# A two-layer recurrent trunk with routed experts: the first expert's rows by a matmul, logits by token tiles, earlier weight loads

## The chip, the core and the metric

The kernel runs on one core of a Trainium2 chip. The metric is the device time of one execution in microseconds. All arithmetic is fp32.

## What is computed

256 prompt tokens and 8 sample tokens, each a row of 1024 values, pass two layers. A layer is a mixer, a LayerNorm, a mixture of experts and another LayerNorm; each sublayer f gives x <- LayerNorm(alpha * x + f(x)). Layer 0's mixer is gated DeltaNet and mLSTM heads with one output projection (w_out); layer 1's is a state-space layer (S5) and a gated linear unit, (g @ A) * sigmoid(g @ B). The experts are:

```
logits = x @ router_w                       # 16 experts
probs = softmax(logits); sel = probs + router_b
grp_score = sum of the top 2 of each group of 4 in sel; best = argmax(grp_score)
idx = top 2 of sel within the best group; wts = probs[idx] / sum
out = sum over experts e of comb[e] * ((silu(x @ gate[e]) * (x @ up[e])) @ down[e])
```

## The kernel before

**Tiles.** Tokens are in three tiles: 0 and 1 (128 rows each, every second token) and TT = 2, the 8 samples. The five engines have programs of their own, at the end of the file, and meet at semaphores.

**Projection and LayerNorm.** In layer 0 `mix_pe_out` (L776) adds the output projection to the scaled residual, tile 0, tile 1 (L804), samples (L816). `ln_dve` (L1418) norms each tile, in that order, on DVE (VectorE); a tile is ready after L1442. In layer 1 `glu_pe` (L2457) computes tile 0, tile 1, then the samples (L2478, both halves of the columns), and `glu_half` takes the halves into the residual.

**Routing.** PE (TensorE) transposes tiles 0 and 1 (`xT_pe`); DVE and ACT (ScalarE) copy them from PSUM. `route_pe` (L1528) then multiplies the router by all 256 columns at once (L1533) into logits with experts on partitions, transposes these back (L1538) and treats the samples apart (L1513, L1541). `route_dve` (L1564) has some 60 small DVE operations in a chain: softmax, best group, first and second expert, the mask of both (L1639). Two matmuls count the tokens ahead in each expert (L1546, L1547). From this come each token's slot (`at_slot`) and list (`in_list`); each expert has a list of up to 64 rows. `list_value` (L1693) goes through a matmul (L1551) into row numbers (`gidx`), and `list_sel` through another (L1556) into the weights of the combination. GpSimd (POOL) copies the normed rows with columns permuted (`rows_pool`, L1716), SyncE stores them to DRAM (L1723), and `pool_gather` (L1903) fetches an expert's rows by an indirect DMA (L1911).

**Experts.** `moe_pe` (L1963) takes the 16 experts in order: gate and up (L1803, L1804, eight chunks each in two passes), the next expert's rows transposed (`pe_tokens`, L1782), the former expert's down projection (L1827), the hidden rows transposed (`pe_units`), and for every second expert the combination (L1845). Before expert 0 it waits for `sel` and puts down tile 0's residual (L1481).

**Weights.** An expert has 4 MB of gate and up weights and 2 MB of down weights. Gate and up have three places, loaded in halves, down two (layer 0) or three (layer 1). SyncE's queue issues the loads in one fixed order and waits in it for the place to be freed: `moe_first_loads` (L2037) and `moe_weights` (L2063). In layer 0 the loads for experts 0 and 1 wait for the samples' projection (the step `mixAB2`), gate and up of expert 3 for expert 0's matmuls, and the third down load for expert 0's down matmuls (`down_done`, L1775). `keep_busy` (L302) issues 512-column matmuls whose results nobody reads.

## Time and profile before

| | us |
|---|---|
| median of 3 runs (1001.24 to 1004.36) | 1003.9 |
| the profiled execution | 1003.38 |
| its span | 1001.6 |
| PE busy | 902.1 (90%) |
| DVE busy | 400.7 (40%) |
| DMA moved | 277.52 MB, 277 GB/s mean |

Busy shares are means over stages. The prediction reads stages by windows, queues and timelines. PEclk is TensorE's granted clock, 1.00 for 2.4 GHz and 0.50 for 1.2 GHz. A PE timeline row merges neighbouring instructions of one line; an fp32 matmul stands as two, called passes here.

### The profile page before, as it was taken

What the parts mean: (1) busy time and instruction counts of PE and PEld (TensorE: products, weight loads), DVE (VectorE), ACT (ScalarE), POOL (GpSimd) and SP (SyncE); (2) the same over time, 40 slices, a digit from 0 to 9 for tenths busy, and PEclk for the clock granted to TensorE, in tenths of its full rate; (3) what the DMA queues carried; (4) which work ended last, traced back from release to release, by engine and by line L of the source; (5) the groups of instructions that cost most, each with busy time, mean ns of one, the idle gap of its engine ahead of it and who ended that gap; (6) DMA issues with size and microseconds to landing.
All of it is one profiled execution on the core that took longest, in us unless ns stands there. A gap on an engine that the chain in (4) does not pass through costs nothing.

```text
span 1001.6 us, 12283 instructions
## 1 busy us (share of the span) xinstructions
PE 902.1 (90%) x4936; PEld 490.6 (49%) x4936; DVE 400.7 (40%) x838; ACT 175.7 (18%) x310; POOL 217.7 (22%) x328
## 2 busy tenths in 40 slices
PE   7999988998984799999899879899749999999993
PEld 5888867996343233333333368744233333333331
DVE  4599507726646022122134279602561121221115
ACT  0402140223010111111011153301301111111011
POOL 4579982401021411101010110100211001111000
PEclk8999997999896899999999999999869999999997
DMA  9446739102769579999999936660479789999982
GB/s 269 106 134 256 261 121 306 67 12 98 258 216 408 200 303 409 406 403 401 410 406 425 419 122 198 207 268 0 190 311 368 307 357 406 397 415 398 417 340 87
DMA packets 83579, 277.52 MB, mean 277 GB/s; under 512 B 25337, under 2 KB 44231, under 8 KB 60854
## 3 DMA queue, kind: packets, MB, share of 16 engines
q1 hardware_dynamic: 70298, 255.86, 66.3%
q10 hardware_dynamic: 10660, 16.49, 5.0%
q0 software_dynamic: 2560, 4.33, 1.5%
q8 instruction: 42, 0.69, 0.3%
q14 instruction: 19, 0.16, 0.0%
HBM read 261.49 MB, written 18.01 MB: 279 GB/s over the span
## 4 chain that ended last, share of the span: by engine, by line
PE 73%; DMA 15%; DVE 7%; ACT 2%; issue 1%; SPq 0%; POOL 0%; DVEq 0%; ACTq 0%; POOLq 0%
PE ps L1803 17%; DMA ring<-in_moe_w_up 13%; PE ps L342 11%; PE ps L1827 8%; PE ps L2471 6%; PE ps L1845 4%; PE ps L804 3%; PE ps L1782 3%; PE ps L2333 1%; PE ps L305 1%; PE ps L633 1%; PE ps L1533 1%; PE ps L650 1%; DMA work<-x_rows,work 1%; PE ps L2348 1%
## 5 line engine op out<-in xcount | busy, mean ns | idle before, releaser
L1803 PE MATMUL ps<-ring,work 128*64 128x512 f32 x480 | 217.3, 605 | 11.4 <-DMA ring<-in_moe_w_up 9.9
L1804 PE MATMUL ps<-ring,work 128*64 128x512 f32 x480 | 217.4, 605 | 0.0
L1803 PEld LDWEIGHTS ps<-ring,work 128*64 128x64 f32 x480 | 63.8, 139 | 137.5 <-issue 121.4
L1887 DVE TENSOR_TENSOR work<-ps,work 64x512 f32<-64x512 f32 x32 | 33.8, 1057 | 223.3 <-ACT work L1858 223.3
L342 PE MATMUL ps<-work,ring 128*128 128x264 f32 x512 | 115.2, 387 | 0.0
L1827 PE MATMUL ps<-ring,work 128*64 128x512 f32 x248 | 113.0, 598 | 1.5 <-DVE work L1892 1.4
L1828 PE MATMUL ps<-ring,work 128*64 128x512 f32 x248 | 113.1, 599 | 0.0
L342 PEld LDWEIGHTS ps<-work,ring 128*128 128x128 f32 x512 | 96.8, 190 | 16.4
L1249 POOL TENSOR_TENSOR ring<-ring 128x512 f32<-128x512 f32 (+5 forms) x76 | 90.5, 1207 | 9.5 <-DVE ring L1245 6.2
L1897 DVE COPY work<-ps 64x512 f32<-64x512 f32 x32 | 22.2, 694 | 149.8 <-PE ps L1828 149.8
L1908 POOL COPY work<-work 64x1 int32<-64x1 int32 x32 | 5.7, 178 | 339.6 <-PE ps L1782 300.0
L1782 PEld LDWEIGHTS ps<-const,work 64*128 64x128 f32 x448 | 39.3, 162 | 52.4 <-issue 44.1
L1804 PEld LDWEIGHTS ps<-ring,work 128*64 128x64 f32 x480 | 63.8, 139 | 0.0
L1845 PE MATMUL ps<-work 128*128 128x512 f32 x128 | 59.5, 605 | 2.0 <-DVE work L1897 1.8
L1858 ACT ACTIVATE work<-ps 64x512 f32<-64x512 f32 x32 | 18.8, 589 | 239.0 <-PE ps L1804 239.0
L2471 PE MATMUL ps<-ring,work 128*128 128x512 f32 x128 | 57.1, 608 | 3.0 <-ACT work L2414 2.1
L1827 PEld LDWEIGHTS ps<-ring,work 128*64 128x64 f32 x248 | 31.4, 136 | 57.5 <-issue 54.0
L1782 PE MATMUL ps<-const,work 64*128 64x64 f32 x448 | 48.2, 246 | 6.3 <-DMA work<-x_rows,work 4.3
L2471 PEld LDWEIGHTS ps<-ring,work 128*128 128x128 f32 x128 | 24.7, 195 | 34.2 <-issue 30.8
L1845 PEld LDWEIGHTS ps<-work 128*128 128x128 f32 x128 | 22.9, 189 | 37.8 <-issue 37.8
L504 DVE SCALAR_TENSOR_TENSOR work<-work 128x256 f32<-128x256 f32 x36 | 40.4, 1123 | 1.3
L1854 ACT COPY work<-ps 128x512 f32<-128x512 f32 x32 | 18.7, 585 | 108.5 <-PE ps L1782 108.5
(491 smaller groups left out, 1187.8 us busy)
## 6 DMA issues: line engine op xcount, KB each, us to landing
ring<-in_moe_w_down SPq DMA_DIRECT2D x31, 2048.0 KB, 17.0
ring<-in_moe_w_gate SPq DMA_DIRECT2D x60, 1024.0 KB, 14.6
ring<-in_moe_w_up SPq DMA_DIRECT2D x60, 1024.0 KB, 16.8
ring<-in_w_in ACTq DMA_DIRECT2D x6, 2048.0 KB, 8.7
s_out_mats<-ring SPq DMA_DIRECT2D x4, 1280.0 KB, 4.7
ring<-in_w_in SPq DMA_DIRECT2D x2, 2048.0 KB, 10.2
s_in_mats<-ring SPq DMA_DIRECT2D x4, 1024.0 KB, 6.3
ring<-in_w_out SPq DMA_DIRECT2D x1, 4096.0 KB, 16.5
```

What stands on the lines that cost most here:

```text
L342: last = nc.tensor.matmul(ps[:, proj_bank(j), 0:T], win[g % 2][:, k, (j % 4) * P:(j % 4 + 1) * P], xT[:, k], start=k == 0, stop=k == DC - 1)
L504: nc.vector.scalar_tensor_tensor(y, raw[:, c, w:w + SEQ], convT[:, c, 24 + w:25 + w], y, ALU.mult, ALU.add).then_inc(*dv.done())
L804: last = nc.tensor.matmul(ps[:, 2 * i + n, :], rows_of(oT[:, k], i), wout[:, k, n * 512:(n + 1) * 512], start=False, stop=k == 7)
L1249: tt = lambda o, a, b, op, name=None: nc.gpsimd.tensor_tensor(o, a, b, op).then_inc(*po.done(name))
L1782: last = op(bank[:, c * SLOT:(c + 1) * SLOT], rows[0:SLOT, c * P:(c + 1) * P], ident[0:SLOT, 0:SLOT], **(dict(start=True, stop=True) if c ...
L1803: nc.tensor.matmul(ps[0:SLOT, 5, :], xgT[s][:, c], gate_w[slot][:, c], start=c == 0, stop=c == DC - 1)
L1804: last = nc.tensor.matmul(ps[SLOT:P, 5, :], xgT[s][:, c], up_w[slot][:, c], start=c == 0, stop=c == DC - 1)
L1827: nc.tensor.matmul(ps[0:SLOT, 7, :], hidT[s][:, c], down_w[l][slot][:, c, 0:512], start=c == 0, stop=c == 3)
L1828: last = nc.tensor.matmul(ps[SLOT:P, 7, :], hidT[s][:, c], down_w[l][slot][:, c, 512:D], start=c == 0, stop=c == 3)
L1845: last = nc.tensor.matmul(ps[:, 2 * i + n, :], S[rows, i * P:(i + 1) * P], y[rows, 512 * n:512 * n + 512], **flags)
L1887: nc.vector.tensor_tensor(hid[s][0:SLOT].rearrange("t (c p) -> t p c", c=4), strided(ps[SLOT:P, 5, :]), strided(sg[s][SLOT:P]), ALU.mult). ...
L2471: last = nc.tensor.matmul(ps[:, banks_ab[ab], :], gyT[:, k, i * P:(i + 1) * P], glu_w(h, k)[:, ab], start=k == 0, stop=k == DC - 1)
```

## The change

- Output projection: tile 0, samples, tile 1. Gated unit: half 0 of tiles 0, 1 and the samples, half 1 of the samples, of tile 0, of tile 1. The norm's order is 0, TT, 1 in layer 0 and TT, 0, 1 in layer 1.
- Logits come per tile, with tokens on partitions: the transposed tile is the stationary operand, the router the moving one. All PSUM copies of the transposed tiles are on ACT. Group scores are the largest of six pair sums.
- Six `keep_busy` matmuls follow the logits, two follow the counts. The counts of tiles ahead are accumulated in PSUM.
- Expert 0's rows are no longer gathered: `pe_first_tokens` multiplies the permuted rows, as POOL leaves them, by a one-hot matrix of its slots (24 matmuls). The gathers start with expert 1. The matmuls of `sel` and tile 0's residual move behind expert 0's gate and up. The largest count goes to `route_sel` behind expert 0's product, too.
- Expert 0's gate and up weights are loaded in four 1 MB pieces, each when the chunks of w_out or of the gated unit's weights that lie there have been used. In layer 1 expert 1's come earlier still.

```
-                        pe_outer(t, 2 + k // 5)
+            residual_pe(t, 0, 0)
+            pe_outer(t, 1)
+            for k in range(8):
+                for n in range(2):
+                    last = nc.tensor.matmul(ps[:, n, :], rows_of(oT[:, k], 0), wout[:, k, n * 512:(n + 1) * 512], start=False, stop=k == 7)
...
+            t.wait_ge(*dv.at("new11"))
+            residual_pe(t, 1, 2)
             t.wait_ge(*dv.at("new15"))
             residual_pe(t, TT, 4)
...
+            for k in range(8):
+                for n in range(2):
+                    last = nc.tensor.matmul(ps[:, 2 + n, :], rows_of(oT[:, k], 1), wout[:, k, n * 512:(n + 1) * 512], start=False, stop=k == 7)
+                if k == 7:
+                    last.then_inc(*pe.done("mixAB1"))
+                elif k % 2 == 1:
+                    last.then_inc(*pe.done(f"wout{k // 2}"))
...
+
...
+        def logits_pe(t, tag, i):
+
+            t.wait_ge(*ac.at(f"{tag}xT_in{i}"))
+            rows = slice(i * P, i * P + tok(i))
+            for k in range(DC):
+                last = nc.tensor.matmul(ps[0:tok(i), 1, i * NE:(i + 1) * NE], xT[:, k, rows], router[:, k], start=k == 0, stop=k == DC - 1)
+            return last
...
         def route_pe(t, tag):
-            t.wait_ge(*ac.at(f"{tag}xT"))
-            t.wait_ge(*dv.at(f"{tag}xT"))
+            xT_pe(t, tag, 0)
+            xT_rest_pe(t, tag)
             t.wait_ge(sem("router_in"), 32)
-            for k in range(DC):
-                last = nc.tensor.matmul(ps[0:NE, 6, 0:SEQ], router[:, k], xT[:, k, 0:SEQ], start=k == 0, stop=k == DC - 1)
-            last.then_inc(*pe.done(f"{tag}logitsT"))
...
-            for k in range(DC):
-                last = nc.tensor.matmul(ps[0:NS, 1, TT * NE:3 * NE], xT[:, k, SEQ:], router[:, k], start=k == 0, stop=k == DC - 1)
-            last.then_inc(*pe.done(f"{tag}logits"))
+            logits_pe(t, tag, 0)
+            logits_pe(t, tag, TT)
+            xT_pe(t, tag, 1)
+            logits_pe(t, tag, 1).then_inc(*pe.done(f"{tag}logits"))
+            keep_busy(0, 6)
             t.wait_ge(*dv.at(f"{tag}mask"))
             flat_mask = rt(9, 48)
...
+            nc.tensor.matmul(ps[:, 1, 0:48], before, flat_mask, start=True, stop=False)
+            t.wait_ge(*dv.at(f"{tag}tiles_so_far"))
+            nc.tensor.matmul(ps[:, 1, 0:48], ones, rt(4, 48), start=False, stop=True).then_inc(*pe.done(f"{tag}pos"))
+            t.wait_ge(*dv.at(f"{tag}all_tiles"))
+            nc.tensor.matmul(ps[:, 6, 256:256 + NE], ones, rt(5, 48)[:, 0:NE], start=True, stop=True).then_inc(*pe.done(f"{tag}total"))
+
+            keep_busy(0, 2)
             t.wait_ge(*dv.at(f"{tag}lists"))
             for n in range(6):
                 last = nc.tensor.matmul(ps[0:SLOT, 1, 128:128 + LISTS], at_slot[:, n], list_value[:, n], start=n == 0, stop=n == 5)
             last.then_inc(*pe.done(f"{tag}lists"))
+
+        def route_sel_pe(t, tag):
+
             t.wait_ge(*dv.at(f"{tag}list_sel"))
...
-            for i, (a, b, op) in enumerate(((0, 1, ALU.max), (0, 1, ALU.min), (2, 3, ALU.max), (2, 3, ALU.min))):
...
+            pair, score = rt(4, 12, 6), rt(13, 48)[:, 0:12]
+            for at, n, step in ((0, 3, 1), (3, 2, 2), (5, 1, 3)):
+                nc.vector.tensor_tensor(pair[:, :, at:at + n], g4[:, :, 0:n], g4[:, :, step:step + n], ALU.add).then_inc(*dv.done())
+            v.wait_ge(*dv.last())
+            red(score, pair, ALU.max).then_inc(*dv.done())
...
-            inside = rt(6, 12, EPG)
-            nc.vector.tensor_copy(inside, g_hot.unsqueeze(2).to_broadcast([P, 12, EPG])).then_inc(*dv.done())
-            v.wait_ge(*dv.last())
-            nc.vector.tensor_tensor(sel, sel, rt(6), ALU.mult).then_inc(*dv.done())
-            nc.vector.tensor_scalar(rt(6), rt(6), 1e30, -1e30, ALU.mult, ALU.add).then_inc(*dv.done())
-            v.wait_ge(*dv.last())
-            nc.vector.tensor_tensor(sel, sel, rt(6), ALU.add).then_inc(*dv.done())
+            outside = rt(5, 48)[:, 0:12]
+            nc.vector.tensor_scalar(outside, g_hot, 1e30, -1e30, ALU.mult, ALU.add).then_inc(*dv.done())
+            v.wait_ge(*dv.last())
+            nc.vector.tensor_tensor(g4, g4, outside.unsqueeze(2).to_broadcast([P, 12, EPG]), ALU.add).then_inc(*dv.done())
...
+            so_far, mask = rt(4), rt(9)
+            nc.vector.memset(so_far[:, 0], 0.0).then_inc(*dv.done())
+            v.wait_ge(*dv.at(f"{tag}mask"))
+            nc.vector.tensor_copy(so_far[:, 1], mask[:, 0]).then_inc(*dv.done())
+            nc.vector.tensor_tensor(so_far[:, 2], mask[:, 0], mask[:, 1], ALU.add).then_inc(*dv.done(f"{tag}tiles_so_far"))
...
+            nc.vector.tensor_tensor(rt(5, 48)[:, 0:NE], so_far[:, 2], mask[:, 2], ALU.add).then_inc(*dv.done(f"{tag}all_tiles"))
...
+                red(at[:, 1, :, j], rt(12 + j), ALU.add).then_inc(*dv.done())
             v.wait_ge(*pe.at(f"{tag}pos"))
-            pos = rt(6)
-            nc.vector.tensor_copy(rt(12, 96), ps[:, 1, 0:96]).then_inc(*dv.done())
-            v.wait_ge(*dv.last())
...
+            pos = ps[:, 1, 0:48].rearrange("p (a b) -> p a b", a=3)
...
             nc.vector.tensor_tensor(list_value, in_list, per_list(value_f), ALU.mult).then_inc(*dv.done(f"{tag}lists"))
...
+            nc.vector.tensor_tensor(first_slots, at_slot,
+                                    in_list[:, :, 0:1].to_broadcast([P, 6, SLOT]), ALU.mult).then_inc(*dv.done())
+            v.wait_ge(*dv.last())
+            nc.vector.tensor_tensor(first_slot[:, :, 0], first_slot[:, :, 0], first_slot[:, :, 1], ALU.add).then_inc(*dv.done(f"{tag}first_slot"))
...
+            route_lists(v, tag)
...
+        def route_sel(v, tag):
+
+            v.wait_ge(*pe.at(f"{tag}total"))
+            nc.vector.tensor_reduce(cnt[:, 0:1], ps[:, 6, 256:256 + NE], AX, ALU.max).then_inc(*dv.done())
+            v.wait_ge(*dv.last())
+            nc.vector.tensor_copy(cnt[:, 1:2].bitcast(I32), cnt[:, 0:1]).then_inc(*dv.done(f"{tag}cnt"))
             v.wait_ge(*pe.at(f"{tag}sel"))
             nc.vector.tensor_copy(sel.rearrange("p a b -> p (a b)"), ps[:, 0, 0:2 * LISTS]).then_inc(*dv.done(f"{tag}sel"))
...
+        def pe_first_tokens(t, tag, l):
+
+            for i in range(3):
+                t.wait_ge(*po.at(f"{tag}rows{i}"))
+            t.wait_ge(*dv.at(f"{tag}first_slot"))
+            for c in range(DC):
+                for i in range(3):
+                    n = tok(i)
+                    last = nc.tensor.matmul(ps[:, 4, c * SLOT:(c + 1) * SLOT], xperm[0:n, i, c * P:(c + 1) * P], first_slot[0:n, i, 0],
+                                            start=i == 0, stop=i == 2)
+            last.then_inc(sem(f"tokens_done{l}"), 1)
+
...
-            pool.wait_ge(*x_ready(tag, 2))
-            for s in range(2):
-                nc.gpsimd.memset(xg[s], 0.0).then_inc(*po.done(f"{tag}xg_zero"))
-            pool.wait_ge(*po.at(f"{tag}xg_zero"))
+            pool.wait_ge(*x_ready(tag, 1))
+            nc.gpsimd.memset(xg[1], 0.0).then_inc(*po.done(f"{tag}xg_zero1"))
+            pool.wait_ge(*po.at(f"{tag}xg_zero1"))
             pool.wait_ge(*dv.at(f"{tag}gidx"))
             pool.wait_ge(sem(f"x_rows{l}"), 48)
-            for k in range(NE):
+            for k in range(1, NE):
+                if k == 2:
+                    pool.wait_ge(*pe.at(f"{tag}sel"))
+                    nc.gpsimd.memset(xg[0], 0.0).then_inc(*po.done(f"{tag}xg_zero0"))
+                    pool.wait_ge(*po.at(f"{tag}xg_zero0"))
                 pool_gather(pool, l, *at_expert(k))
...
-            t.wait_ge(*dv.at(f"{tag}sel"))
-            residual_pe(t, 0, 0)
-            pe_tokens(t, l, *at_expert(0))
+            pe_first_tokens(t, tag, l)
             for k in range(NE):
                 pe_gate_up(t, l, *at_expert(k))
+                if k == 0:
+                    route_sel_pe(t, tag)
                 if k % 2 == 1 and k >= 3:
                     pe_combine(t, l, k // 2 - 1, k - 2, slice(0, P), (k // 2 - 1) % 2)
...
+                if k == 0:
+                    t.wait_ge(*dv.at(f"{tag}sel"))
+                    residual_pe(t, 0, 0)
...
+            a.wait_ge(*dv.at(f"{tag}list_sel"))
...
+        def first_gate_up(q, l, freed):
+
+            for part, (dst, name) in enumerate(((gate_w[0], "moe_w_gate"), (up_w[0], "moe_w_up"))):
+                for half in range(2):
+                    q.wait_ge(*freed[2 * part + half])
+                    cols = slice(half * 4 * FF, (half + 1) * 4 * FF)
+                    q.dma_start(dst.rearrange("p k f -> p (k f)")[:, cols].unsqueeze(1),
+                                io[name][l].rearrange("e (p k) f -> p e (k f)", p=P)[:, 0:1, cols]).then_inc(sem(f"w_gu{half}0_{l}"), 16)
+
         def moe_first_loads(q, l):
...
                 gate_up_load(q, l, *load_of(2))
             else:
-                q.wait_ge(*pe.at("glu2"))
-                gate_up_load(q, l, *load_of(0))
+                q.wait_ge(*pe.at(f"glu0{TT}"))
                 gate_up_load(q, l, *load_of(1))
+                first_gate_up(q, l, [pe.at(f"glu_b{min(b, 2)}") for b in range(4)])
+                q.wait_ge(*pe.at("glu11"))
+                down_load(q, l, *load_of(1))
                 route_loads(q, "n2", l)
-                down_load(q, l, *load_of(1))
-                q.wait_ge(*pe.at("n2sel"))
+                q.wait_ge(*pe.at("n2logits"))
                 q.wait_ge(sem("stores_s5"), 16 * 2 * (NS + 1))
                 down_load(q, l, *load_of(2))
...
+            glu_tile_pe(t, 0, 0)
+            s5_state_pe(t)
+            glu_tile_pe(t, 0, 1)
+            glu_samples_pe(t, 0)
+            for b in range(4):
+                t.wait_ge(sem(f"glu_in1{b}"), 64)
+            t.wait_ge(*ac.at("tanh00"))
+            glu_samples_pe(t, 1)
+            t.wait_ge(*ac.at("s5_states"))
+            glu_tile_pe(t, 1, 0)
+            t.wait_ge(*dv.at("prod00"))
+            glu_tile_pe(t, 1, 1)
...
+            ln_root(act, "n0", 0)
             act.wait_ge(*pe.at("mixAB2"))
             sample_rows(act, "n0", 4)
             ln_root(act, "n0", TT)
-            xT_copy(act, ac, nc.scalar.copy, "n0", 1)
+            ln_root(act, "n0", 1)
+            xT_copy(act, "n0", 0)
+            xT_rest_copy(act, "n0")
+            xT_copy(act, "n0", 1)
...
+            for i in ROWS["n2"]:
+                glu_act(act, 1, i)
                 ln_root(act, "n2", i)
-            xT_copy(act, ac, nc.scalar.copy, "n2", 1)
+            xT_copy(act, "n2", 0)
+            xT_rest_copy(act, "n2")
+            xT_copy(act, "n2", 1)
...
+            ln_dve(dve, "n0", 1, in_banks, mixed, ROWS["n0"])
             route_dve(dve, "n0")
-            route_lists(dve, "n0")
```

## Rows read from the trace of the kernel before

**Rows 1.** Windows: start:end, length, busy (x instructions) per engine, PEclk, DMA share, GB/s.

```profile
326.00:339.00 13.00, 8.42 (x31) 3.19 (x31) 0.00 (x0) 1.87 (x2) 6.49 (x15) 0.74 0.15 45
...
350.50:356.00 5.50, 5.50 (x32) 2.03 (x28) 1.07 (x1) 1.18 (x2) 1.32 (x3) 1.00 0.15 50
...
371.00:552.00 181.00, 174.42 (x860) 64.90 (x856) 48.30 (x84) 21.02 (x36) 13.18 (x30) 0.99 1.01 408
...
808.00:965.00 157.00, 153.42 (x768) 57.43 (x766) 28.50 (x44) 19.27 (x33) 11.84 (x27) 1.00 1.01 405
```

**Rows 2.** SyncE's queue in layer 0: start us, us, line, transfer.

```profile
291.68 0.35 SPq L1766 DMA_DIRECT2D ring<-in_moe_w_gate  x1
...
338.74 0.33 SPq L1766 DMA_DIRECT2D ring<-in_moe_w_gate  x1
...
356.01 0.33 SPq L1776 DMA_DIRECT2D ring<-in_moe_w_down  x1
```

**Rows 3.** PE in layer 0: start us, us, line, operation, count, idle before.

```profile
273.61 13.90 PE L804 MATMUL ps<-ring,work 128*128 128x512 f32 x32
...
297.43 6.44 PE L1533 MATMUL ps<-work,fix 128*16 128x256 f32 x16 [3.48 <-ACT work L2163]
303.81 0.66 PE L1513 MATMUL ps<-const,work 8*128 8x8 f32 x8
...
304.79 0.56 PE L1541 MATMUL ps<-fix,work 128*8 128x16 f32 x16
313.64 0.66 PE L1546 MATMUL ps<-work,fix 128*128 128x48 f32 x2 [8.30 <-DVE work L1639]
...
319.78 1.73 PE L1551 MATMUL ps<-work 128*64 128x80 f32 x11 [5.04 <-DVE work L1693]
...
332.82 1.11 PE L1803 MATMUL ps<-ring,work 128*64 128x512 f32 x1 [0.68 <-ACT work L1854]
...
344.50 0.64 PE L1803 MATMUL ps<-ring,work 128*64 128x512 f32 x1
```

**Rows 4.** PE: the first gate matmul of layer 1's first expert.

```profile
752.13 0.64 PE L1803 MATMUL ps<-ring,work 128*64 128x512 f32 x1 [0.68 <-ACT work L1854]
```

**Rows 5.** DVE in layer 0, the same columns.

```profile
268.49 4.22 DVE L994 SCALAR_TENSOR_TENSOR ring<-ring,work,ps 128x128 f32<-128x128 f32 x16 [2.21 <-PE ps L772]
...
290.58 1.29 DVE L1442 SCALAR_TENSOR_TENSOR work<-work 128x1024 f32<-128x1024 f32 x1
...
313.38 0.21 DVE L1639 TENSOR_TENSOR work<-work,fix 128x48 f32<-128x48 f32 x1
...
319.06 0.66 DVE L1693 TENSOR_TENSOR work<-work,fix 128x480 f32<-128x480 f32 x1
```

**Rows 6.** Windows of the granted clock, columns as in the first group.

```profile
296.20:303.00 6.80, 5.57 (x14) 2.01 (x15) 2.53 (x5) 1.75 (x2) 3.80 (x3) 0.51 1.01 424
303.00:306.00 3.00, 2.24 (x30) 1.40 (x28) 1.12 (x6) 0.00 (x0) 0.00 (x0) 0.97 1.02 429
307.00:323.00 16.00, 4.31 (x29) 4.15 (x31) 13.11 (x70) 0.00 (x0) 0.36 (x2) 0.50 1.01 400
...
719.40:726.20 6.80, 4.99 (x12) 1.80 (x13) 3.06 (x6) 1.71 (x2) 3.67 (x3) 0.52 1.01 426
```

**Rows 7.** The chain of waits in time: start us, us, what.

```profile
177.78 0.89 PE ps L646 x8
...
598.94 5.20 PE ps L305 x12
```

**Rows 8.** PE: the first gate matmul of layer 1's second expert.

```profile
761.60 0.64 PE L1803 MATMUL ps<-ring,work 128*64 128x512 f32 x1
```

**Rows 9.** Gathers of both layers, issue to landing.

```profile
DMA to landing us min/median/max: 3.0/7.3/10.1
```

**Rows 10.** PE in layer 1: the gated unit's samples, the last logits.

```profile
706.23 7.05 PE L2478 MATMUL ps<-ring,work 128*8 128x512 f32 x64
...
728.30 0.56 PE L1541 MATMUL ps<-fix,work 128*8 128x16 f32 x16
```

225 lines of the change are left out of this document (88 added, 137 removed).

## The prediction

> **What bounds the kernel now.** I read four views. First the windows, to see which resource is full in each stage of the experts. In layer 0 the DMA engines are idle from 326 to 339 us and nearly so from 350.5 to 356, and then full for 181 us at 408 GB/s, while PE is busy 174.4 of the 181; in layer 1 they are full from 808 to 965 [rows 1]. So the late part of both layers is set by the stream of weights, and PE has only a few us to spare: both must come forward for the end to come forward.
>
> Then SyncE's queue, to see what starts that full stream. In layer 0 expert 3's first half is issued at 338.74, after half of expert 0's gate and up, and the third down load at 356.01, after expert 0's down matmuls; from there the stream never stops [rows 2]. In layer 1 the full stretch begins at 808 [rows 1] in the same way, with a load that waits for a half of the fifth expert's gate and up. Neither start is set by the first loads, which are issued at 291.68 [rows 2] and have landed by 326 [rows 1]. Both are set by when PE begins the experts. The time to shorten is therefore from the last norm to the first gate matmul, which runs at 332.82 [rows 3] and 752.13 [rows 4]; a us saved there moves PE and the stream alike.
>
> Last the timelines of PE and DVE in between. Tile 1 is normed at 291.87 [rows 5], the logits end at 305.35 (304.79 + 0.56) [rows 3], the mask at 313.59, `list_value` at 319.72 [rows 5]; then come the list matmuls, the gather and the transposes. The granted clock is 0.51 in 296.2:303 and 0.50 in 307:323, where PE does little [rows 6].
>
> **Prices.** A pass with a 128-column stationary tile and few moving columns is 0.111 us at full clock (0.89 / 8) [rows 7]; two at half clock take 0.66 with their drain [rows 3], and I take twice the warm price, 0.22. A 512-column pass is 0.433 (5.20 / 12) [rows 7]. Eight passes with 8 contraction rows take 0.57 (303.81 to 304.38, 0.66 with the drain) [rows 3] at clock 0.97 [rows 6]: 0.071 each. A dependent DVE step is 0.19 (13.11 / 70) [rows 6], one that follows without a wait about 0.1.
>
> The trace thus makes a load with 8 rows cheaper than one with 128. The Trainium skill says otherwise (TensorE: Matmul & The Clock Gate, LDWEIGHTS): load time goes by columns, not by contraction rows, P / 1.2, so 107 ns either way. By that page the 16 sample passes of the new product cost an estimated 1.7 instead of 1.1 us, and the result is 1.2 us later over both layers. I stay with the row.
>
> **Layer 0, part by part.**
> 1. Order of the projection. The same matmuls run: samples between the tiles, tile 1 last. Tile 1's 13.90 us [rows 3] now end where the samples did, at 291.6 (their step released the issue at 291.68) [rows 2]. Its norm took 4.4 us (287.51 to 291.87) [rows 3, 5], so it is ready at 296.0. The wait for `new15`, now ahead of the samples, costs nothing: those states were done at 272.71 (268.49 + 4.22) [rows 5], before tile 1's matmuls began.
> 2. Logits. Tile 0's and the samples' transposes, copies and logits (copies behind tile 1's root on ACT) hold PE to about 297.2. Then 8 transposes (1.0), ACT's copies (0.7) and 16 passes at 0.111 (1.8): 300.8 instead of 305.35, a gain of 4.5. It replaces the 6.44 us product at half clock [rows 3]. Bounds: at half clock 304.4 to 305; nothing gained, nothing lost.
> 3. DVE to the mask. Nine small operations become four, four become two: three dependent steps and four followers fewer, 0.95 us. Before it took 8.24 (305.35 to 313.59) [rows 3, 5]; the mask M comes at 300.8 + 7.3 = 308.1. Six `keep_busy` matmuls are 12 x 0.433 = 5.2 us and end at 306, under the mask's cover. At half clock they would be 10.4 and 3 us late: a bound, and part of a rival.
> 4. Mask to lists, 6.13 before [rows 5]. Nine steps and five followers leave the path (2.2), about 0.9 comes (running sums, count matmuls): 4.8.
> 5. Lists to the first gate matmul, 13.1 before (319.72 to 332.82) [rows 3, 5]. Now: 12 list passes at half the former 0.144 (1.73 / 12) [rows 3], 0.9 us; `first_slot` (two DVE operations, about 0.8) under them; the product, 32 x 0.111 + 16 x 0.071 = 4.7; drain and ACT copy 0.8 (0.68 idle before) [rows 3]. Sum 6.4 with one wait more, and the gate starts at M + 11.2 = 319.3 instead of 332.82. Its weights are there: the initial loads ended at 326 with 12.6 MB, those of expert 0 in the first third, and their pieces now start up to 10 us earlier.
> 6. Expert 0's turn. At full clock it takes 9.47 (752.13 to 761.60) [rows 4, 8]. The moved `sel` matmuls add some 1.6 and tile 0's residual 4 x 0.433 = 1.7; a wait of 1.0 for the hidden rows becomes one of 0.7 for the transposed rows. That is 12.5, against 11.68 here before (332.82 to 344.50, clock low at first) [rows 3]. Expert 1 starts at 331.8 instead of 344.5: **12.7 us earlier.**
>
> What queues behind: DVE does `route_lists`, `weight` and `list_sel` by M + 9, before the first hidden product. POOL's memset for expert 2 waits for `sel`, so that gather is issued some 10.5 us after the first gate matmul and lands after 7.3 (10.1 at most) [rows 9]; it is needed at 19.4, 1.6 us to spare. The S5 work on POOL stays behind it, the gather of expert 3 has over 3 us. On SyncE the pieces precede the row stores, but these wait for tile 1's norm anyway and gather 1 for `gidx`.
>
> **Layer 1.** The gated unit ends as before near 713.3 (706.23 + 7.05) [rows 10], now with tile 1: after tanh and two products (2.0, an estimate from DVE's 0.66 for 480 columns) [rows 5] and the 4.4 of the norm it is ready at 719.9. Tile 0's copies wait for tile 1's root on ACT, to 718.5. PE idles from 715 as before, and then the clock fell (0.52 in 719.4:726.2) [rows 6]; I take half clock to 726: logits of tile 0 3.6, of the samples 0.6, transposes 1.5, copies 0.7, tile 1's logits 1.8 to 3.6. They end at 726.7 (bounds 724.5 and 728.5) instead of 728.86 [rows 10]. M = 734.0, first gate matmul 745.2, expert 1 at 757.7 instead of 761.6: **3.9 us earlier**, less than in layer 0 since the gather was short here and expert 0's turn grows by 3.0. The earlier weight loads I cost at nothing: they were covered.
>
> **Sum.** 1003.38 - 12.7 - 3.9 = 986.8 for the profiled execution. The median of the runs is 0.5 above it: 987.0.
>
> **Rivals.**
> - *Half clock from the lists on, in one layer.* The gaps between the mask, `keep_busy` and lists let the clock fall. Lists cost 0.9 more, the product 5.0, expert 0's turn 2.2 (11.68 - 9.47) [rows 3, 4, 8]: 8.1, so 995. For: it fell in each such stretch before. Against: the eight extra matmuls, and gaps of about 2 us. Chance 0.12; in both layers 1003, chance 0.04.
> - *Slower.* `keep_busy` itself starts at half clock and the clock does not return before the gate matmuls. Then in layer 0 the logits end at 305.4, the mask waits for the six (10.4 us), lists at 320.5, product at 333, so nothing is gained, and the longer turn loses 3; in layer 1 the same sum loses 8 to 9. 1015. It decides once the cold stretch costs over 16.6 us in all. Against: in 296.2:303 and 719.4:726.2 [rows 6] the clock came back once PE was busy for some us. Chance 0.05.
> - *The gather of expert 2 is late*, at 10.1 us or more, in one or both layers: 2 to 4 us, 990. Chance 0.07.
> - *Layer 1's logits run at full clock:* 2.2 more, 984.8. Chance 0.06.
> - *The stream does not follow.* If its full stretch were tied to the first loads, only their 10 us lead would count. But it had 18 us of idle time before 356 [rows 1]; inside the forecast's range.
>
> **How the numbers follow.** Forecast 0.66, with 983 to 991 as its own range (DVE steps, passes and turn each to 1 us a layer). The range asked for reaches down to layer 1 at full clock, 982, and up to one cold layer, 996. A measurement tells about 0.3% (3 us) from no change. Faster: 0.66 + 0.12 + 0.07 + 0.06 = 0.91; the same 0.04; slower 0.05.
>
> **What would show it.** Right: first gate matmuls near 319 and 745 with 0.64 us each instead of 1.11; clock 1.00 from `keep_busy` on; the third down load of layer 0 issued near 343.5; the full stretches as long as now; 32 gathers become 30. Wrong: half clock in the product, PE waiting for a gather or for `sel` in expert 0's or 1's turn, or an end of layer 0 that moves less than its first expert.

## The result and the profile after

The changed kernel takes 1009.0 us (median of 5 runs, 1007.67 to 1010.84), the kernel before 1003.35 (5 runs): ratio 1.0068, 95% interval 1.0046 to 1.0091. It is slower by 5.6 us where 987.0 was forecast. The profiled execution took 1009.0 us with a span of 1007.3 (before: 1003.38 and 1001.6).

PE in layer 0 of the changed kernel, from its timeline (start us, us, line, operation, count, idle before). L1506 are the transposes of tile 0 (at 288.33) and of tile 1 (at 294.21), L1522 logits, L305 `keep_busy`, L1557 lists, L1798 the new product, L1819 and L1820 gate and up, L1565 `sel`, L1482 tile 0's residual:

```profile
288.33 1.04 PE L1506 MATMUL ps<-const,work 128*128 128x128 f32 x8
...
294.21 1.97 PE L1506 MATMUL ps<-const,work 128*128 128x128 f32 x8
296.86 3.59 PE L1522 MATMUL ps<-fix,work 128*128 128x16 f32 x16 [0.68 <-ACT work L1529]
300.29 8.22 PE L305 MATMUL ps<-const 128*128 128x512 f32 x12
...
312.42 1.04 PE L1557 MATMUL ps<-work 128*64 128x80 f32 x12 [1.53 <-DVE work L1673]
313.40 11.21 PE L1798 MATMUL ps<-work 128*128 128x64 f32 x48
325.29 1.12 PE L1819 MATMUL ps<-ring,work 128*64 128x512 f32 x1 [0.68 <-ACT work L1870]
...
334.47 1.81 PE L1565 MATMUL ps<-work 128*64 128x160 f32 x24
...
337.85 0.59 PE L1786 MATMUL ps<-const,work 64*128 64x64 f32 x5 [0.77 <-ACT work L1870]
338.37 1.98 PE L1482 MATMUL ps<-work,const 128*128 128x512 f32 x4
...
340.29 0.64 PE L1819 MATMUL ps<-ring,work 128*64 128x512 f32 x1
```

The same view in layer 1:

```profile
722.45 3.59 PE L1522 MATMUL ps<-fix,work 128*128 128x16 f32 x16 [0.68 <-ACT work L1529]
...
738.70 12.75 PE L1798 MATMUL ps<-work 128*128 128x64 f32 x48
752.13 1.12 PE L1819 MATMUL ps<-ring,work 128*64 128x512 f32 x1 [0.68 <-ACT work L1870]
...
767.04 0.64 PE L1819 MATMUL ps<-ring,work 128*64 128x512 f32 x1
```

The product takes 11.21 and 12.75 us instead of the forecast 4.7, and the gate matmuls after it start at 1.12 us, where those of layer 1 started at 0.64 before [rows 4]. The windows of the changed kernel (start:end, length, busy of PE, PEld, DVE, ACT and POOL, PEclk, DMA share, GB/s) say why. The stretches are tile 1's logits, the product's first 2 us, its last 8.6 us and the first gate matmuls; then layer 1's product:

```profile
296.80:300.30 3.50, 3.44 (x17) 3.44 (x17) 0.00 (x0) 1.77 (x3) 0.00 (x0) 0.50 0.99 417
...
313.40:315.40 2.00, 2.00 (x14) 1.73 (x14) 1.79 (x10) 0.00 (x0) 0.04 (x1) 1.00 0.98 414
316.00:324.60 8.60, 8.60 (x32) 7.30 (x32) 0.25 (x1) 0.00 (x0) 1.50 (x2) 0.51 0.10 31
...
325.20:330.00 4.80, 4.71 (x12) 1.48 (x14) 0.00 (x0) 0.04 (x1) 0.00 (x0) 0.51 0.00 0
...
738.00:751.50 13.50, 13.45 (x60) 11.45 (x57) 3.28 (x14) 0.01 (x1) 2.12 (x3) 0.55 0.04 12
```

The granted clock is 1.00 when the product begins and 0.51 from 316 on, though PE's records fill the stretch: 8.60 of 8.60 us. It is the level of 1.2 GHz, and it stays through the first five of the sixteen passes each of gate and up. The Trainium skill (TensorE: Matmul & The Clock Gate, in the table of clock states) gives that level to an idle or cold array. By PE's records this trace does not agree. But the ends of matmuls are modelled in these records, and a pass stands for 0.27 us here (8.60 / 32) where one at full clock can take 0.115, so a filled row does not show that the array itself had no pauses.

Where the time went, by stretches between two marks of each layer (the forecast is for the distance, so that the start of the layer, which is 3.65 us earlier in this execution, does not count):

| stretch, us | before | forecast | after |
|---|---|---|---|
| L0: last projection matmul to expert 1 | 52.9 | 40.2 | 52.3 |
| L1: gated unit's end to expert 1 | 48.4 | 44.5 | 56.5 |
| expert 1 of L0 to gated unit's end | 368.7 | 368.7 | 370.2 |
| expert 1 of L1 to the span's end | 240.0 | 240.0 | 240.3 |

That is -0.6, +8.1, +1.5 and +0.3, with -3.65 for the earlier start: +5.7 on the spans, as measured. The earlier start is no gain of the change: tile 0's first transpose comes anywhere from 287.7 to 292.2 us in the traces of the experiments, whose matmuls up to there are the same. The weight stream did follow PE: the third down load of layer 0 is issued at 351.79, 11.50 us after expert 1's first matmul, as it was before (11.51) [rows 2, 3].

### The profile page after: what moved, and what is told of

Its sections match the earlier page's. It is cut to its first block, busy times and chain, and to the rows that moved or that the text cites. A ratio compares the mean times of both kernels' runs of the same rounds, so it can differ in the third digit from the quotient of the medians.

```text
span 1007.3 us, 12686 instructions
## 1 busy us (share of the span) xinstructions
PE 941.0 (93%) x5142; PEld 523.4 (52%) x5142; DVE 396.7 (39%) x820; ACT 178.5 (18%) x318; POOL 216.6 (22%) x322
## 4 chain that ended last, share of the span: by engine, by line
PE 79%; DMA 11%; DVE 5%; ACT 2%; issue 1%; SPq 0%; POOL 0%; DVEq 0%; ACTq 0%
PE ps L1819 19%; PE ps L342 11%; DMA ring<-in_moe_w_up 11%; PE ps L1843 8%; PE ps L2500 6%; PE ps L1861 4%; PE ps L1786 3%; PE ps L1798 2%; PE ps L305 2%; PE ps L1522 1%; PE ps L800 1%; PE ps L2367 1%; PE ps L816 1%; PE ps L1482 1%; PE ps L633 1%; PE ps L650 1%
## 5 line engine op out<-in xcount | busy, mean ns | idle before, releaser
L1819 PE MATMUL ps<-ring,work 128*64 128x512 f32 x480 | 219.5, 610 | 12.0 <-DMA ring<-in_moe_w_up 10.6
L1820 PE MATMUL ps<-ring,work 128*64 128x512 f32 x480 | 219.6, 610 | 0.0
L1819 PEld LDWEIGHTS ps<-ring,work 128*64 128x64 f32 x480 | 64.3, 140 | 141.3 <-issue 124.8
L1820 PEld LDWEIGHTS ps<-ring,work 128*64 128x64 f32 x480 | 64.3, 140 | 0.0
L1786 PE MATMUL ps<-const,work 64*128 64x64 f32 x430 | 45.8, 244 | 1.5 <-ACT work L1870 1.5
L305 PE MATMUL ps<-const 128*128 128x512 f32 x72 | 40.7, 710 | 2.9 <-POOL const L267 2.9
## 6 DMA issues: line engine op xcount, KB each, us to landing
ring<-in_moe_w_gate SPq DMA_DIRECT2D x60, 1024.0 KB, 14.3
```

The costliest lines, as they stand in the source:

```text
L305: nc.tensor.matmul(ps[:, bank, :], ident, ident.unsqueeze(1).to_broadcast([P, 4, P]), start=True, stop=True)
L1786: last = op(bank[:, c * SLOT:(c + 1) * SLOT], rows[0:SLOT, c * P:(c + 1) * P], ident[0:SLOT, 0:SLOT], **(dict(start=True, stop=True) if c ...
L1819: nc.tensor.matmul(ps[0:SLOT, 5, :], xgT[s][:, c], gate_w[slot][:, c], start=c == 0, stop=c == DC - 1)
L1820: last = nc.tensor.matmul(ps[SLOT:P, 5, :], xgT[s][:, c], up_w[slot][:, c], start=c == 0, stop=c == DC - 1)
```

## The experiments

Twelve kernels ran, each beside the kernel before on the same chip (its medians there: 1002.18, 1003.37, 1002.89 and 1003.35), so ratios are compared, and a difference from the changed kernel is that of the two ratios, in us of 1003.35. The intervals are 2 to 6 us wide on either side. Two distances are read from each trace: G, from tile 0's first transpose (tile 0's logits begin with it) to expert 0's first gate matmul, and T, from there to expert 1's. Each pair is layer 0 / layer 1. In e1_gather, e2_wide, e7_warm to e10_turn_warm and e12_late_loads two more things differ from the changed kernel: `list_sel` lies elsewhere, and layer 1's third down load follows expert 3's gate and up loads. Neither was measured alone.

| kernel | us | ratio [95%] | G | T |
|---|---|---|---|---|
| changed | 1009.0 | 1.0068 [1.0046, 1.0091] | 36.96 / 41.59 | 15.00 / 14.91 |
| e1_gather | 1003.33 | 1.0027 [1.0009, 1.0044] | 32.95 / 37.44 | 15.41 / 14.78 |
| e2_wide | 994.3 | 0.9927 [0.9900, 0.9954] | 30.39 / 33.60 | 14.43 / 14.42 |
| e3_no_keep | 1015.99 | 1.0141 [1.0113, 1.0170] | 40.12 / 43.34 | 15.03 / 15.24 |
| e4_two_tiles | 991.89 | 0.9903 [0.9871, 0.9934] | 29.05 / 32.65 | 12.74 / 12.74 |
| e5_dummies | 1001.05 | 1.0003 [0.9974, 1.0031] | 36.82 / 39.95 | 12.74 / 12.74 |
| e6b_order | 994.77 | 0.9925 [0.9895, 0.9954] | 30.89 / 34.87 | 14.43 / 14.35 |
| e7_warm | 994.96 | 0.9918 [0.9888, 0.9948] | 30.40 / 32.70 | 14.43 / 14.12 |
| e8_sel_gaps | 996.5 | 0.9944 [0.9925, 0.9963] | 30.62 / 33.72 | 14.31 / 14.28 |
| e9_turn | 987.81 | 0.9871 [0.9828, 0.9914] | 30.62 / 33.97 | 10.23 / 10.23 |
| e10_turn_warm | 986.95 | 0.9846 [0.9806, 0.9886] | 29.88 / 31.05 | 10.23 / 10.22 |
| e11_rows128 | 992.7 | 0.9897 [0.9855, 0.9939] | 30.80 / 34.75 | 12.74 / 14.44 |
| e12_late_loads | 987.14 | 0.9852 [0.9793, 0.9911] | 29.90 / 30.88 | 11.57 / 10.23 |

**The product undone alone (e1_gather).**

```diff
-            for k in range(1, NE):
...
+            for k in range(NE):
                 pool_gather(pool, l, *at_expert(k))
...
-            pe_first_tokens(t, tag, l)
+            pe_tokens(t, l, *at_expert(0))
```

> The changed kernel with one part undone: expert 0's rows come by the gather again (memset, gather, transposes), everything else stays; list_sel lies elsewhere and layer 1's third down load follows expert 3's gate and up load. In the changed kernel the product is busy for 11.2 us in layer 0 and 12.7 us in layer 1, mostly at a granted clock of 0.50, and gate matmuls start 12.9 and 14.4 us after list_value. Theory A (the product in narrow passes is the loss: its passes neither are cheap nor keep the clock up): layer 0 is about level, since its gather took 7.3 us, and layer 1 wins 3 to 5 us, since its gather took 3.7: 1004 to 1006. Theory B (the loss is elsewhere, in the deferred sel matmuls or the order of the gated unit): no change, 1008 to 1010.

1003.33: by the ratios 4 us below the changed kernel, and still 1 to 4 us above the kernel before. The product is worse than the gather it replaces, in both layers (G is 4.0 and 4.2 us shorter here), where theory A had layer 0 level. The rest of the change does bring the gate forward: from the last projection matmul to the first gate matmul it is 33.4 us in layer 0 instead of 41.3, and from the gated unit's end 37.4 in layer 1 instead of 38.9. The turn of expert 0 gives that back: 15.41 and 14.78 us instead of 11.68 and 9.47 [rows 3, 4, 8], with the moved `sel` and residual in it and the clock at 0.50 in its first 4 us in both layers. The lists and first gate in layer 0, and two windows of gate matmuls:

```profile
315.41 1.04 PE L1557 MATMUL ps<-work 128*64 128x80 f32 x12 [1.37 <-DVE work L1673]
322.65 1.43 PE L1786 MATMUL ps<-const,work 64*128 64x64 f32 x9 [6.19 <-DMA work<-x_rows,work]
324.76 1.11 PE L1819 MATMUL ps<-ring,work 128*64 128x512 f32 x1 [0.67 <-ACT work L1870]
```

```profile
324.70:329.00 4.30, 4.24 (x10) 1.24 (x12) 0.00 (x0) 0.01 (x1) 3.73 (x9) 0.50 0.09 25
745.80:750.00 4.20, 4.12 (x10) 1.24 (x12) 0.00 (x0) 0.02 (x1) 0.96 (x1) 0.50 0.10 28
```

**The samples' third of the product left out (e4_two_tiles).** Only tiles 0 and 1 are summed, so rows of samples are missing from expert 0's input.

```diff
-                for i in range(3):
+                for i in range(2):
...
-                                            start=i == 0, stop=i == 2)
+                                            start=i == 0, stop=i == 1)
```

> The changed kernel without the samples' third of the product, 16 passes with 8 contraction rows a layer (expert 0 then gets zero rows in place of sample tokens; that part is left out). If such a pass costs what a 128-row pass costs in this stage, near 0.27 us at half clock, the two layers lose 8 to 9 us: 1000 to 1001. If it costs the 0.071 us that I took from the transposes of the samples, 2 to 3 us: 1006 to 1007.

991.89, 17 us below the changed kernel: far more than expected of the 16 passes in each layer. Timeline and windows of that kernel (product, then gate):

```profile
316.60 3.79 PE L1798 MATMUL ps<-work 128*128 128x64 f32 x32
321.06 0.64 PE L1819 MATMUL ps<-ring,work 128*64 128x512 f32 x1 [0.68 <-ACT work L1870]
```

```profile
316.60:320.40 3.80, 3.78 (x33) 3.64 (x32) 2.61 (x11) 0.00 (x0) 1.51 (x3) 1.00 0.69 289
321.00:325.00 4.00, 3.94 (x20) 1.38 (x22) 0.00 (x0) 0.00 (x1) 0.00 (x0) 1.00 0.15 47
```

The 32 passes with 128 rows cost 0.115 us each (3.79 less the last one's drain, by 32), the price I had given them (0.111), and the clock stays up, also in the gate matmuls. So the eight-row passes have a part in its fall, or the mere number of passes has; e6b_order decides between the two.

**Wide matmuls in the product (e5_dummies).** One 512-column matmul, read by nothing, after every second chunk.

```diff
+                if c % 2 == 0:
+                    keep_busy(0, 1)
```

> The changed kernel with work added: one 512-column matmul that nobody reads after every second chunk of the product, 4 a layer, 0.87 us each at full clock. Theory A (the narrow passes let the clock fall, and the fall is the loss): the clock holds at 1.00, a pass costs 0.14 instead of 0.27 and the first gate matmuls 0.64: product and dummies take about 10 us instead of 11.2 and 12.7, the turn of expert 0 2.2 less, so 6 to 9 us less in all, 1000 to 1003, although work is added. Theory A2 (number of passes, whatever the clock): 7 us more, 1015 to 1017.

1001.05: with 3.8 us of extra work in each layer (4 times 318.89 - 317.93) it is 6.5 us faster than the changed kernel. The clock is 1.00 throughout (layer 0's window), and the timeline shows what an eight-row pass costs at that clock:

```profile
314.00:325.00 11.00, 11.00 (x60) 7.99 (x58) 2.85 (x13) 0.00 (x0) 2.05 (x3) 1.00 0.29 113
```

```profile
316.14 1.86 PE L1798 MATMUL ps<-work 128*128 128x64 f32 x12
317.93 1.12 PE L305 MATMUL ps<-const 128*128 128x512 f32 x2
318.89 1.86 PE L1798 MATMUL ps<-work 128*128 128x64 f32 x12
...
325.99 0.64 PE L1821 MATMUL ps<-ring,work 128*64 128x512 f32 x1 [0.68 <-ACT work L1872]
```

Twelve passes, 8 with 128 rows and 4 with 8, take 317.93 - 316.14 = 1.79 us. With 8 x 0.115 that leaves 0.22 for each of the four: twice a 128-row pass. (The excess can as well lie in the 128-row pass behind it; the sum is the same.) So there are two costs, the pass itself and the clock that goes with it.

**The same passes in another order (e6b_order).** The samples' eight matmuls come last instead of between the chunks. All chunks then share one accumulation group of the bank, so the start and stop flags change along with the order.

```diff
-            for c in range(DC):
-                for i in range(3):
+            for i in range(3):
+                for c in range(DC):
                     n = tok(i)
...
-                                            start=i == 0, stop=i == 2)
+                                            start=(i, c) == (0, 0), stop=(i, c) == (2, DC - 1))
```

> The 48 matmuls of the product of the changed kernel in another order: all chunks of tile 0, all of tile 1, then the samples' eight with 8 rows, instead of tile 0, tile 1, samples for each chunk. Same work. Theory A (the eight-row passes cost 0.22 us and more where each stands between 128-row ones, and the clock falls with them): the product takes 4.8 to 5.5 us, at granted clock 1.00 as with the samples left out (3.79 us there), and the time is 993 to 997. Rival (it is the amount of narrow passes that the clock falls with, and leaving the samples out only took a third of it): the product still takes 9 to 12 us at clock 0.5 and the time is 1005 to 1009.

994.77, and theory A's numbers. Its timeline, and its windows over the 128-row passes and the eight-row ones:

```profile
314.54 5.71 PE L1798 MATMUL ps<-work 128*128 128x64 f32 x48
320.93 0.64 PE L1819 MATMUL ps<-ring,work 128*64 128x512 f32 x1 [0.68 <-ACT work L1870]
```

```profile
314.50:318.30 3.80, 3.76 (x33) 3.69 (x33) 1.00 0.69 289
318.30:320.30 2.00, 1.95 (x17) 1.81 (x16) 1.00 0.35 98
```

(These columns are busy of PE and PEld for the product's line alone.) In a row, a pass with 8 rows costs what one with 128 does: 1.95 / 17 and 3.76 / 33 are both 0.114 to 0.115. The order, with its flags, is worth 14 us.

But T is 14.43 and 14.35 here, not the 12.74 of e4_two_tiles. The clock falls after all, behind the product, in the gate matmuls of both layers, also in layer 0, whose first one still takes 0.64 us:

```profile
322.00:326.00 4.00, 4.00 (x14) 1.27 (x12) 0.00 (x0) 0.00 (x0) 0.00 (x0) 0.62 0.00 0
...
738.20:742.00 3.80, 3.79 (x10) 1.15 (x12) 0.00 (x0) 0.00 (x0) 0.00 (x0) 0.57 0.00 0
```

**The same order with 128 rows (e11_rows128).** The changed kernel's own order, but the samples' block is taken over 128 rows, of which 120 are zero.

```diff
+                if i == TT:
+                    nc.gpsimd.memset(xperm[:, i], 0.0).then_inc(*po.done(f"{tag}rest_zero"))
...
-                    n = tok(i)
+                    n = P
```

> The changed kernel with the samples' 16 passes of the product taken over 128 rows instead of 8 (rows 8 to 127 are zero), in the changed kernel's own order: tile 0, tile 1, samples for each chunk. More rows, same number of passes, same order. Theory A (what costs is the change between 8 and 128 rows from pass to pass, and it takes the clock along): the product takes 5.6 to 5.8 us at clock 1.00 as with the samples last (5.71), first gate matmul as there: 994 to 997. Rival (it is what order of chunks and tiles does to PSUM or the weights, rows have no part in it): 11 us and half clock as in the changed kernel: 1006 to 1010.

992.7. Sixteen times the rows in the samples' passes, and 17 us faster than the changed kernel; layer 0's product and gate:

```profile
316.71 5.57 PE L1801 MATMUL ps<-work 128*128 128x64 f32 x48
322.96 0.64 PE L1822 MATMUL ps<-ring,work 128*64 128x512 f32 x1 [0.68 <-ACT work L1873]
```

```profile
316.70:322.30 5.60, 5.59 (x50) 5.43 (x48) 2.63 (x11) 0.00 (x0) 2.34 (x3) 1.00 0.61 243
322.90:327.00 4.10, 4.04 (x20) 1.47 (x22) 0.00 (x0) 0.01 (x1) 0.00 (x0) 1.00 0.01 1
```

Order and flags are the changed kernel's here, and the product costs nothing extra in either layer; in e6b_order the 8 rows are there, and it costs nothing extra either. So it is 8-row and 128-row passes in turn.

**The product turned round (e2_wide).** The slots stand as weights (64 columns), the rows stream by in 512 columns: 6 matmuls, then copies by ACT and DVE and 8 transposes.

```diff
-                    last = nc.tensor.matmul(ps[:, 4, c * SLOT:(c + 1) * SLOT], xperm[0:n, i, c * P:(c + 1) * P], first_slot[0:n, i, 0],
...
+                    last = nc.tensor.matmul(ps[SLOT * h:SLOT * h + SLOT, 7, :], first_slot[0:n, i, 0], xperm[0:n, i, 512 * h:512 * h + 512],
```

> The changed kernel with the product turned round: the one-hot slots are the stationary operand (64 columns), the rows the moving one (512 columns), 6 matmuls instead of 24; the 64 rows are copied to where a gather would put them and transposed as for the other experts. No memset for expert 2. Theory A (clock): wide passes keep the clock at 1.00 through the first gate matmuls (0.64 us each, not 1.1); gate starts near 11 us after the mask instead of 17.5 and 18.9, expert 0's turn is 12.5 instead of 15: 18 us less in all, 989 to 993. Theory A2 (only the number of passes counts, the clock falls anyway): about 11 to 13 us less, 996 to 998, first gate matmuls still near 1.1 us. Theory B (elsewhere): over 1005.

994.3. The product takes 2.94 us in 12 passes, the copies and transposes give back what it saves against 5.71: G is 0.5 and 1.3 us below that of e6b_order. The 8-row passes stand last here too. The time falls between the ranges of the first two theories: the product runs at clock 1.00, but wide passes did not keep the clock in the gate. Over 4 us of gate matmuls from 320 it is 0.70, and T is 14.4 in both layers instead of the expected 12.5.

**Without keep_busy (e3_no_keep).**

```diff
-            keep_busy(0, 6)
...
-            keep_busy(0, 2)
```

> The changed kernel without its eight keep_busy matmuls per layer (they compute nothing that is used). Theory A (they hold the clock up from the logits' end to the product's first us, but their end is late by 0.5 us in layer 0): lists and the whole product at half clock, mask to lists unchanged, 1 to 2 us longer per layer less 0.5: 1009 to 1012. Rival (they bring nothing, since the product loses the clock anyway, or they delay): 1007 to 1009.

1015.99, 7 us above the changed kernel, more than either theory said: without them the clock does not come back before the gate, and the whole product runs at the lower level.

```profile
312.16 1.86 PE L1555 MATMUL ps<-work 128*64 128x80 f32 x12 [3.16 <-DVE work L1671]
313.95 13.35 PE L1796 MATMUL ps<-work 128*128 128x64 f32 x48
```

```profile
307.00:327.00 20.00, 16.30 (x66) 14.25 (x66) 8.18 (x38) 0.00 (x0) 2.05 (x3) 0.50 0.44 179
```

**Wide matmuls around the logits (e7_warm), on e2_wide.**

```diff
+            spare = 0 if tag == "n0" else 3
+            keep_busy(spare, 3)
             t.wait_ge(sem("router_in"), 32)
             logits_pe(t, tag, 0)
+            keep_busy(spare, 1)
             logits_pe(t, tag, TT)
+            keep_busy(spare, 1)
             xT_pe(t, tag, 1)
+            keep_busy(0, 1)
```

> The kernel with the product turned round (994.3), plus three wide matmuls that nothing reads before tile 0's logits (in its wait for the copies, 1.25 us in layer 0 and 3.6 us in layer 1), one after each of tile 0's and the samples' logits, one after tile 1's transposes. Theory A (the logits run at half clock only because PE did little and narrow work before; wide work brings the clock back): logits passes at 0.11 to 0.12 us instead of 0.224, the logits' end 1 us later to 1 earlier in layer 0, 2 to 3 us earlier in layer 1: 991 to 994. Rival (the clock does not come back in that time): six matmuls at 0.85 to 0.9 us each, half of them in waits, 2 to 3 us lost per layer: 998 to 1000.

994.96, no different from e2_wide. The logits do run at full clock (16 passes in 1.96 instead of 3.6 us), but the added matmuls take as long as they save: G is the same in layer 0 and 0.9 us shorter in layer 1.

**`sel` into two waits (e8_sel_gaps), on e2_wide.** Half of the `sel` matmuls stand behind the product, half behind the transposes.

```diff
             last.then_inc(*pe.done(f"{tag}first_rows"))
+            route_sel_pe(t, tag, 0)
...
             to_features(ps[:, 4], xg[0], DC, sem(f"tokens_done{l}"))
+            route_sel_pe(t, tag, 1)
...
-                if k == 0:
-                    route_sel_pe(t, tag)
```

> The kernel with the product turned round (994.3), with the sel matmuls taken out of expert 0's turn (1.74 us there) and put, half each, into the two waits for the copies of the first rows (0.89 and 0.67 us). Theory A (deferred work lay on the path to expert 1): expert 0's turn 1.7 us shorter, the first gate matmul at most 0.2 us later per layer: 991 to 992, and no more half clock at the gate matmuls if short waits made it fall, 0.5 to 1 us more. Rival (the turn's end is set by something else, the third expert's gather or the loads): 994.

996.5, and T stays 14.3: on the time the first theory failed. One half of it came true, though. With the waits filled, the gate matmuls run at full clock in both layers, and gate and up take 7.0 us instead of the 8.6 in e2_wide:

```profile
318.40:325.30 6.90, 6.90 (x36) 2.13 (x30) 0.00 (x0) 0.00 (x0) 6.45 (x13) 1.00 0.41 119
...
738.20:745.20 7.00, 7.00 (x36) 2.25 (x32) 0.00 (x0) 0.00 (x0) 0.95 (x1) 1.00 0.38 109
```

What this and the removed `sel` saved was lost again behind the gate. DVE and PE now wait there for ACT (timelines of the three engines):

```profile
325.50 1.28 ACT L1881 ACT_TABLE_LOAD   x1 [7.31 <-PE ps L1827]
326.80 0.59 ACT L1881 ACTIVATE work<-ps 64x512 f32<-64x512 f32 x1
...
327.42 1.04 DVE L1910 TENSOR_TENSOR work<-ps,work 64x512 f32<-64x512 f32 x1 [10.93 <-ACT work L1881]
...
328.51 0.62 PE L1788 MATMUL ps<-const,work 64*128 64x64 f32 x5 [2.30 <-DVE work L1910]
329.14 3.63 PE L1482 MATMUL ps<-work,const 128*128 128x512 f32 x4
```

The table load of silu stands behind the gate's end. In the kernel before it ran at 332.78, under the gate matmuls; the change put a second wait of ACT (for `list_sel`) ahead of it, and in the changed kernel it runs at 334.73, behind the gate. The deferred `sel` had only filled the wait that this makes, and after 2.30 us without work for PE the residual runs at half clock (3.63 us for four, against 1.98).

**The turn put in order (e9_turn), on e8_sel_gaps.** ACT's wait goes ahead of its copy, `sel` is read ahead of the hidden product, the residual fills the wait for the units.

```diff
+            a.wait_ge(*dv.at(f"{tag}list_sel"))
             act_tokens(a, l, *at_expert(0))
-            a.wait_ge(*dv.at(f"{tag}list_sel"))
...
+                if k == 0:
+                    t.wait_ge(*dv.at(f"{tag}sel"))
+                    residual_pe(t, 0, 0)
                 pe_units(t, l, *at_expert(k))
-                if k == 0:
-                    t.wait_ge(*dv.at(f"{tag}sel"))
-                    residual_pe(t, 0, 0)
```

> The kernel with the product turned round and sel in the waits for the copies (996.5), whose expert 0 then has PE wait 2.3 us for the hidden rows. Three things are moved there: ACT waits for list_sel ahead of its xgT copy, so that the table load of 1.28 us runs under the gate matmuls; DVE takes sel out ahead of expert 0's hidden product; tile 0's residual (1.98 us, it ran at half clock in 3.6) stands ahead of expert 0's units, in the wait. Theory A (the deferred work cost nothing where it covered that wait; the turn is bound by the chain gate end, table, silu, hidden product, units): expert 0's turn falls from 14.3 to 11 to 11.8 us, 2.5 to 3.3 us a layer: 988 to 991. Rival (expert 1's own inputs are late next, its tokens or its weights): 993 to 996.

987.81; T is 10.23 in both layers, 4.1 shorter: the wait of 2.3 us is gone, and the residual takes 1.98 instead of 3.63. The three moves were not measured apart. The table load now runs at 318.23, under the gate matmuls, and PE has no idle time left between gate and expert 1:

```profile
325.30:328.60 3.30, 3.30 (x22) 1.93 (x20) 1.06 (x1) 1.18 (x2) 2.85 (x13) 1.00 1.01 427
```

**And with wide matmuls in the logits' waits (e10_turn_warm), on e9_turn.** Those of e7_warm without the two between the logits.

> The kernel before it in this list, plus three wide matmuls that nothing reads ahead of tile 0's logits and one after tile 1's transposes (not the two between, which cost 1.6 to 2 us in the run with six). Theory A (tile 1's logits then run at full clock, 1.8 instead of 3.6 us, and the matmuls stand mostly in waits): 1 us earlier in layer 0, 2 us in layer 1: 986 to 988. Rival (without the two between, the clock still falls in the logits, and their place in the gap costs as much as it gives): within 1 us of the kernel before it.

986.95. G is 0.7 and 2.9 us shorter than in e9_turn, the logits of tile 1 run at clock 1.00 in both layers:

```profile
298.20:300.10 1.90, 1.90 (x17) 1.80 (x17) 0.00 (x0) 1.82 (x3) 0.00 (x0) 1.00 1.02 431
714.00:715.70 1.70, 1.70 (x17) 1.66 (x15) 0.00 (x0) 0.64 (x1) 0.00 (x0) 1.00 0.43 174
```

In layer 0 the clock falls again ahead of the lists, whose matmuls take 1.9 us there instead of 1.04, which takes part of that gain back. On the time it can't be told from e9_turn: the intervals overlap, and the two profiled executions differ by 2.3 us in when they reach tile 0's first transpose. Both beat the kernel before and the changed one.

**Early weight loads undone (e12_late_loads), on e10_turn_warm.**

```diff
-                first_gate_up(q, l, [pe.at("wout0"), pe.at("wout1"), pe.at("wout2"), pe.at("mixAB1")])
+                first_gate_up(q, l, 4 * [pe.at("mixAB1")])
...
-                first_gate_up(q, l, [pe.at(f"glu_b{min(b, 2)}") for b in range(4)])
+                first_gate_up(q, l, 4 * [pe.at("glu11")])
```

> The fastest kernel so far (986.95) with one part of the change undone: all four pieces of expert 0's gate and up weights wait until tile 1's last matmul (projection in layer 0, gated unit in layer 1) instead of each for the chunk whose place it takes. Theory A (the pieces were covered by 25 us or more until the first gate matmul, so that part was worth nothing): 986.5 to 988. Rival (the full stretch of the weight stream, or the third expert's loads queued behind, follow these first loads): 2 to 8 us later, 989 to 995.

987.14, the same, though the interval is wide enough for 6 us either way. Expert 0's weights were in time. In layer 0 PE waited 1.27 us for expert 1's gather, with the DMA engines full until then, and T is 1.3 us longer (11.57): the early loads were worth that much there, below what the time can resolve.

## Why the prediction was wrong

The steps of the working that failed are "Prices" with 5, then 6 and 2. The rest held nearly, and each failed term has its size in the traces.

1. **Price of the eight-row passes and the product (steps "Prices" and 5).** The step said 32 x 0.111 + 16 x 0.071 = 4.7, with the 0.071 from eight transposes with 8 rows in a row. The 0.111 was right (0.115). The 0.071 does not carry over: matmul passes with 8 rows cost 0.115 in a row and 0.22 between 128-row ones (e6b_order, e5_dummies). The Trainium skill (TensorE: Matmul & The Clock Gate, LDWEIGHTS) has the load go by columns, not by contraction rows; for passes in a row this case's trace agrees (0.115 with 8 rows as with 128), against the row I stayed with. Its price would have changed the result by 1.2 us only. What I had no price for was the alternation: with it the product took 11.21 and 12.75 us instead of some 5.6. Of the excess 1.7 is the pass itself (16 x (0.22 - 0.115)), and what is left, 3.9 and 5.4 us, I put down to half clock. Short by 6.5 and 8.0 us.
2. **Clock in the gate matmuls (step 6).** 12.5 for expert 0's turn was right at full clock: 12.74 in e4_two_tiles and e5_dummies. In the changed kernel it is 15.0 and 14.9, since the first five of sixteen passes each of gate and up run at half clock (0.51 in layer 0). Short by 2.5 and 2.4. The alternation is not the only way to this: with it gone, in e6b_order and e2_wide, the turn still takes 14.4. Half clock in the gate goes away only where the short waits between product and gate are filled (e8_sel_gaps and the kernels built on it), or, without an explanation, in e4_two_tiles, e5_dummies and layer 0 of e11_rows128. The 12.5 itself was not a floor either: it held 1.8 us of `sel` and a wait of 0.77, and in e9_turn, with `sel` in the waits ahead of the gate and the table load under it, both are gone from the turn (10.23). I had named ACT's copy there, not its table load.
3. **Clock in the logits (step 2, and layer 1).** The 16 passes of tile 1, costed at 0.111 each, took 3.59 at clock 0.50, 1.8 us more; in layer 0 the eight transposes ahead of them took 1.97 instead of 1.0 as well. The bound named it (304.4 to 305); I took the other end. Short by 3.2 in layer 0 and 2.0 in layer 1.

Together 12.2 and 12.4 us, against 12.1 and 12.0 that the two layers fell short of their forecast.

What held in the changed kernel: the mask at 7.33 us after the logits (7.3), the lists 4.6 after it (4.8; 307.78 to 312.37), the third down load that follows PE, the earlier weight loads worth little (by e12_late_loads 1.3 us in layer 0, nothing in layer 1), the gather of expert 2 in time. The six `keep_busy` took 8.22 instead of 5.2 us, ending 0.5 after the mask, and are worth 7 us. e10_turn_warm measures 986.95 where 987.0 was forecast, but that agreement is in part luck. Its turn is 2.3 us shorter a layer than the 12.5, and its logits need added matmuls that take up part of their gain. Layer 1 is 3.2 us shorter than forecast (41.3 from the gated unit's end to expert 1 instead of 44.5), while the stretch from expert 1 of layer 0 to the gated unit's end takes 373.1 us, 4.4 more than the 368.7 that the forecast kept. What was won ahead of that stretch was thus not passed on in full, and no run looked for the reason.

Of the rivals, *half clock from the lists on* in both layers (1003, given 0.04) was nearest in mechanism (the 1009.0 lies midway between its 1003 and the 1015 of *slower*), but it was not quite what happened: the clock did come back, in `keep_busy`, and the lists ran at full clock (1.04 us). It fell inside the product. The *slower* rival (0.05) had the sign and the threshold, not the place: the three terms cost 24 us over both layers, some 20 of it half clock, against the 16.6 from which it was to decide. My argument against it was that the clock returns once PE is busy for some us. It did return, in `keep_busy`; what the argument left out is that it can fall again while PE's records show it busy.

**Open:** what in the alternation takes the clock down. The runs show that it does, that 128-row passes of the same size and number don't, and that one wide matmul in every twelve passes prevents it. No counter here shows more. Also open is why the clock falls for some 3 us in the gate of e2_wide and e6b_order (both layers) and of e11_rows128 (layer 1), behind a product at 1.00, and stays in layer 0 of e11_rows128 and in e4_two_tiles. Filling the waits between product and gate prevented it in e8_sel_gaps, tried with the turned product only. Nor were the earlier loads, the order of the projection and the new logits each taken out of the changed kernel alone.

## What to carry to other kernels

A remainder tile with few rows does not belong inside the accumulation loop beside full tiles: put it last, or pad it with zeros to the full height. These were worth 14 and 17 us here, over two products of 48 passes each, one a layer. Price a product by rows of its own shape and neighbours, and take the granted clock as a result of what PE does, not of how full its busy row looks. Short waits ahead of a run of matmuls are a good place for deferred matmuls: in e8_sel_gaps they cost 0.2 us there and gate and up became 1.6 us shorter. Where work is deferred past a wait, look at what else the wait now stands ahead of, table loads too.
